# Expert results of a decoder layer: rows scattered by token on GpSimd's queue, or blocks of rows written on the weight queue and gathered at the end

## The reference, cut to what matters

```python
e_idx, gate = route(xf, w_router, b_router)      # 2 of 32 experts per token, all in one group of 4
h = jax.nn.silu(xb @ w_gate[e]) * (xb @ w_up[e])  # per expert, 1024 -> 512
y = h @ w_down[e]                                 # 512 -> 1024
y = segment_sum(y * row_gate[:, None], row_tok)   # each token: the sum of its two experts' rows
x = layer_norm(DEEPNORM_ALPHA * x + y, ln_g[l, 2], ln_b[l, 2])
```

## Time and profile before

| | |
|---|---|
| time, median of 3 runs | 1139.21 us (1138.52 to 1142.39) |
| span of the profiled execution (its first to its last instruction) | 1135.4 us; its time with what lies around the span isn't given apart |
| TensorE busy | 1058.4 us, 93% of the span |
| DVE, ACT, POOL busy | 345.5, 273.6, 85.8 us |
| SP's queue (q1) | 252.81 MB |
| POOL's indirect DMAs (q0) | 8.40 MB |
| HBM read, written | 257.60 MB, 13.05 MB |

### The profile page before, as it was taken

How to read it: one execution, slowest core, us unless ns; L and a number is a source line. 1 busy time by engine, 2 the same in 40 slices (tenths; PEclk the granted TensorE clock), 3 DMA queues, 4 the chain that set the end, 5 groups by cost and what they waited for, 6 DMA issues and landing times.

```text
span 1135.4 us, 15981 instructions
## 1 busy us (share of the span) xinstructions
PE 1058.4 (93%) x6710; PEld 533.3 (47%) x6710; DVE 345.5 (30%) x729; ACT 273.6 (24%) x540; POOL 85.8 (8%) x133
## 2 busy tenths in 40 slices
PE   9999999999899999999998999999998898898896
PEld 4444455566655544566446544444443333333332
DVE  0179522334664453104146211111111011011116
ACT  2431122234454500023202211222111011011123
POOL 2000100000000000100000211111111101101110
PEclk9999999999999999999999899999999989989999
DMA  8112220222024320923316999999999999999996
GB/s 278 37 41 86 97 76 2 76 76 76 14 64 149 110 77 1 361 84 117 148 74 257 368 398 404 403 394 393 393 396 392 401 395 394 399 396 401 398 401 251
DMA packets 55847, 263.31 MB, mean 232 GB/s; under 512 B 7250, under 2 KB 8402, under 8 KB 30944
## 3 DMA queue, kind: packets, MB, share of 16 engines
q1 hardware_dynamic: 49424, 252.81, 57.8%
q0 software_dynamic: 5120, 8.40, 2.3%
q10 hardware_dynamic: 1232, 1.07, 0.3%
HBM read 257.60 MB, written 13.05 MB: 238 GB/s over the span
## 4 chain that ended last, share of the span: by engine, by line
PE 31%; DMA 24%; DVE 3%; issue 1%; ACT 1%; SPq 0%; POOLq 0%; ACTq 0%; DVEq 0%
DMA ring<-in_w_exp_up 7%; PE cpair L2020 5%; PE bank L2030 5%; PE tpair L2020 4%; DMA ar<-in_w_exp_up 3%; PE bank L1861 2%; PE bank L1841 2%; DMA mixT<-in_w_exp_down 2%; DMA ring<-in_w_exp_down 2%; DMA avq<-in_w_exp_up 2%; PE tpair L1861 1%; PE bank L1834 1%; PE cpair L1861 1%; PE tpair L1841 1%; PE cpair L1841 1%; DMA mixT<-y_rows 1%
## 5 line engine op out<-in xcount | busy, mean ns | idle before, releaser
L2020 PE MATMUL cpair<-ring,xgT 128*64 128x512 f32 x312 | 82.8, 594 | 7.6 <-DMA ring<-in_w_exp_up 4.4
L2234 ACT ACTIVATE hs<-cpair 64x512 f32<-64x512 f32 x21 | 12.4, 589 | 237.7 <-PE cpair L2020 237.7
L2464 DVE SCALAR_TENSOR_TENSOR ye<-bank,tabs,xgt 128x512 f32<-128x512 f32 x30 | 22.5, 751 | 136.0 <-PE bank L2030 136.0
L2030 PE MATMUL bank<-ring,hT 128*64 128x512 f32 x224 | 57.6, 656 | 6.2 <-DVE hT L2454 6.2
L2450 DVE TENSOR_TENSOR hs<-cpair,hs 64x512 f32<-64x512 f32 x21 | 14.6, 693 | 154.3 <-ACT hs L2234 154.3
L922 PE MATMUL bank<-xT,ring 128*128 128x512 f32 x128 | 60.9, 606 | 0.0
L1776 POOL DMA_INDIRECT y_rows<-ye,tabs x30 | 30.3, 1011 | 383.8 <-DVE ye L2464 383.8
L2020 PEld LDWEIGHTS cpair<-ring,xgT 128*64 128x64 f32 x312 | 26.2, 137 | 53.1 <-issue 52.0
L365 PE MATMUL bank<-xT,ring 128*128 128x512 f32 x112 | 48.5, 593 | 0.0
L2241 ACT ACTIVATE xgt<-xgt,tabs 64x512 f32<-64x512 f32 x64 | 46.0, 719 | 1.6
L2020 PE MATMUL tpair<-ring,xgT 128*64 128x512 f32 x152 | 39.5, 594 | 4.5 <-DMA ring<-in_w_exp_up 2.5
(11 more groups left out here) (471 smaller groups left out, 1894.7 us busy)
## 6 DMA issues: line engine op xcount, KB each, us to landing
ring<-in_w_exp_gate SPq DMA_DIRECT2D x30, 1024.0 KB, 11.1
ring<-in_w_exp_down SPq DMA_DIRECT2D x30, 1024.0 KB, 11.1
ring<-in_w_exp_up SPq DMA_DIRECT2D x28, 1024.0 KB, 11.2
ring<-in_w_in SPq DMA_DIRECT2D x6, 2048.0 KB, 8.1
ring<-in_w_mem_kv SPq DMA_DIRECT2D x4, 2048.0 KB, 10.3
mixT<-in_w_exp_down SPq DMA_DIRECT2D x7, 1024.0 KB, 10.3
ar<-in_w_exp_down SPq DMA_DIRECT2D x7, 1024.0 KB, 11.0
xT<-in_w_exp_gate SPq DMA_DIRECT2D x6, 1024.0 KB, 11.5
```

The lines of the kernel that those rows point to most:

```text
L2020: last = nc.tensor.matmul(bank[b][m * CAP:(m + 1) * CAP, :], xgT[:, k, :], w(m, h)[:, j * DE:(j + 1) * DE], start=(k == 0), stop=(k == KT ...
L2030: last = nc.tensor.matmul(bank[b][m * CAP:(m + 1) * CAP, :], ht[:, k, :], w(2, h)[:, o:o + 512], start=(k == 0), stop=(k == FT - 1))
```

## The change

The result of an expert no longer goes to the rows of its tokens. The 64 rows of expert e go as they are, empty slots too, to rows 64e to 64e+63 of a table `y_first` in DRAM, by two direct DMAs on SP's queue (`result_out`, 64 partitions x 512 values each, 256 KB together). They are issued in SP's loop over the pieces: the result of e-1 after the piece that takes the place of the third piece of expert e, that is after piece 6e+2+23. The result of 26 is the last in the loop; those of 27, 28 and 29 follow the loop. y_out now counts 32 for each result. The token's own rows of the last two experts go the same way (`token_rows_out`).

At the end POOL gathers the two rows of each token: eight indirect DMAs of 128 rows of 4 KB, by an index `slot_at` = 64 x expert + place (plus a term for further passes, if there were any), which DVE computes during routing. SP only loads the norm's parameters. The table `tabs` becomes `toks` and `gates`; the column of rows goes, and the factor ALPHA is now carried through the one-hot products instead of being derived from the row.

```diff
-        def row_and_gate_columns(pe, ls):
+        def gate_columns(pe, ls):
...
-        def rows_and_gates_read(dve, ls, n):
+        def gates_read(dve, to, n):
             dve.wait_ge(tab_full, 2 * n)
-            nc.vector.tensor_scalar(tabs[:, :, 1], bank[7][:, 0:NE], ls.row_off[:, 0:1], None, ALU.add)
-            nc.vector.tensor_scalar(tabs[:, :, 3].bitcast(F32), bank[7][:, 0:NE], 2.0 * S - 2.0 * OFF, ALPHA, ALU.is_lt,
-                                    ALU.mult)
-            nc.vector.tensor_copy(tabs[:, :, 2].bitcast(F32), bank[7][:, NE:2 * NE]).then_inc(tabs_done, 1)
+            nc.vector.tensor_copy(to[:, :, :].rearrange("p f e -> p (f e)"), bank[7][:, 0:2 * NE]).then_inc(tabs_done, 1)
...
         def rows_out(eng):
             for s in range(2):
-                eng.wait_ge(y_out[s], 16 * (LAST - 1) // 2)
+                eng.wait_ge(y_out[s], 32 * (LAST - 1) // 2)
...
+                    def result_out(e):
+                        sp.wait_ge(y_scaled, e + 1)
+                        for h in range(2):
+                            sp.dma_start(y_first[e * CAP:(e + 1) * CAP, h * 512:(h + 1) * 512], ye[half[h], e % 2, :])\
+                                .then_inc(y_out[e % 2], 16)
+                    def token_rows_out(e):
+                        sp.wait_ge(x_done, 2 * (e + 1))
+                        for h in range(2):
+                            sp.dma_start(y_first[e * CAP:(e + 1) * CAP, h * 512:(h + 1) * 512], xrow[half[h], e % 2, :])\
+                                .then_inc(late_out, 16)
+                    sent = 0
...
                         sp.wait_ge(w_read, read_at[e, DN if i == 2 else GU, h])
                         piece_here(sp, n - 4)
                         load_piece(sp, n)
+                        if i == 0 and h == 1 and sent < e < LAST:
+                            result_out(e - 1)
+                            sent = e
+                    for e in range(sent, LAST - 1):
+                        result_out(e)
...
-                    rows_out(sp)
-                    sp.wait_ge(late_out, 32)
+                    for e in PE_LAST:
+                        token_rows_out(e)
                     down_read(sp, LAST - 2)
                     sp.wait_ge(f_end, more * NE + 1)
-                    for t in range(NT):
-                        if t == 2:
-                            for h, src in enumerate((ln_g, ln_b)):
-                                sp.dma_start(ln3[:, h, :], src[0, 2:3, :].to_broadcast([P, D])).then_inc(n3.here, 16)
-                        sp.dma_start(yb[t], y_v[t * P:(t + 1) * P, :, :]).then_inc(y_read[t], 16)
+                    for h, src in enumerate((ln_g, ln_b)):
+                        sp.dma_start(ln3[:, h, :], src[0, 2:3, :].to_broadcast([P, D])).then_inc(n3.here, 16)
...
                     for e in range(LAST - 1):
                         rows_in(e + 2)
-                        pool.wait_ge(y_scaled, e + 1)
-                        scatter(tabs[:, e, 1:2], ye[:, e % 2, :]).then_inc(y_out[e % 2], 16)
...
-                    further_blocks(pool, before, body)
-                    for e in PE_LAST:
-                        pool.wait_ge(x_done, 2 * (e + 1))
-                        scatter(tabs[:, e, 1:2], xrow[:, e % 2, :]).then_inc(late_out, 16)
+                    further_blocks(pool, before, body, after)
+                    rows_out(pool)
+                    pool.wait_ge(late_out, 64)
+                    down_read(pool, LAST - 2)
+                    for t in range(NT):
+                        for k in range(TOP_K):
+                            r = k * NT + t
+                            collect(yb[t][:, k, :], y_first[:, :], SLOTS, slot_at[:, r:r + 1]).then_inc(y_read[t], 16)
...
@@ routing, DVE
                     dve.wait_ge(oh_both, 2)
+                    link(dve, V.tensor_tensor(ohr[:, :, :, :], oh[:, 0:TOP_K, :, :],
+                                              ls.erow[:, :].unsqueeze(1).unsqueeze(1).to_broadcast(wide), ALU.mult))
+                    link(dve, V.tensor_reduce(slot_f[:, :], ohr[:, :, :, :].rearrange("p k t e -> p (k t) e"), AX_X,
+                                              ALU.add))
                     dve.wait_ge(rk_full, 1)
...
-                    tokens_read(dve, 1)
+                    rows = TOP_K * NT
+                    link(dve, V.tensor_tensor(past[:, :, :], ls.thresholds[:, :].unsqueeze(1).to_broadcast([P, rows, S // CAP - 1]),
+                                              ls.place[:, :].unsqueeze(2).to_broadcast([P, rows, S // CAP - 1]), ALU.is_le))
+                    link(dve, V.tensor_tensor(slot_f[:, :], slot_f[:, :], ls.place[:, :], ALU.add))
+                    tokens_read(dve, toks, 1)
+                    link(dve, V.tensor_reduce(blk_of[:, :], past[:, :, :], AX_X, ALU.add))
+                    link(dve, V.scalar_tensor_tensor(slot_at[:, :], blk_of[:, :], float(NE * CAP - CAP), slot_f[:, :], ALU.mult,
+                                                     ALU.add))
...
@@ experts, DVE
                         if e >= 2:
-                            dve.wait_ge(y_out[e % 2], 16 * (e // 2))
+                            dve.wait_ge(y_out[e % 2], 32 * (e // 2))
```

More of the change, by code:

```diff
@@ L1387, in hybrid_decoder_trunk @@
         class Lists:
-            KEPT = 905
+            KEPT = 904
             def __init__(self, flat):
@@ L1404, in hybrid_decoder_trunk @@
         lists_out, lists_back, asked = sem("lists_out"), sem("lists_back"), sem("asked")
-        tabs = sb("tabs", [P, NE, 4], I32)
+        toks = sb("toks", [P, NE], I32)
+        gates = sb("gates", [P, 2, NE])
         hits_done, tab_full, tabs_done = sem("hits_done"), sem("tab_full"), sem("tabs_done")
@@ L1566, in hybrid_decoder_trunk @@
         combT = sb("combT", [P, 2, S])
-        y_rows = nc.dram_tensor("y_rows", (TOP_K * S * 2, D // 2), F32, kind="Internal").ap()
+        SLOTS, FURTHER = NE * CAP, (S // CAP - 1) * NE * CAP
+        y_first = nc.dram_tensor("y_first", (SLOTS, D), F32, kind="Internal").ap()
+        y_further = nc.dram_tensor("y_further", (FURTHER, D), F32, kind="Internal").ap()
+        y_half_rows = y_further.rearrange("r (h c) -> (r h) c", h=2)
         n3 = Norm(2)
@@ L1595, in hybrid_decoder_trunk @@
         ls2 = Lists(free[8])
+        toks2 = free[9][:, 0:NE].bitcast(I32).rearrange("p (e i) -> p e i", i=1)
+        gates2 = free[9][:, NE:3 * NE].rearrange("p (f e i) -> p f e i", f=2, i=1)
         acc = ((6, 7), (3, 1), (2, 4), (5, 0))
@@ L1607, in rows_out, with further_blocks @@
             for s in range(2):
-                eng.wait_ge(y_out[s], 16 * (LAST - 1) // 2)
-        def further_blocks(eng, before, body):
+                eng.wait_ge(y_out[s], 32 * (LAST - 1) // 2)
+        def further_blocks(eng, before, body, after=None):
             n = eng.value_load(more_i[0:1, 0:1], min_val=0, max_val=S // CAP - 1)
@@ L1616, in further_blocks @@
                     body(blk)
+                if after:
+                    after()
             return n
@@ L1689, in before @@
                         sp.dma_start(ls2.kept, kept_rows[:, :]).then_inc(lists_back, 16)
+                        sp.wait_ge(f_cleared, 1)
+                        for b in range(S // CAP - 1):
+                            sp.dma_start(y_further[b * NE * CAP:(b + 1) * NE * CAP, :].rearrange("(r p) c -> p r c", p=P),
+                                         xf.unsqueeze(1).to_broadcast([P, NE * CAP // P, D])).then_inc(f_zero, 16)
+                        sp.wait_ge(f_zero, 16 * (S // CAP - 1))
                     def body(blk):
@@ L1781, in rows_in @@
                         pool.wait_ge(x_done, 2 * (e - 1))
-                        gather(xg[half[e % 2], :], tabs[0:CAP, e, 0:1]).then_inc(xg_here[e % 2], 16)
-                    gather(xg[half[1], :], tabs[0:CAP, 1, 0:1]).then_inc(xg_here[1], 16)
+                        gather(xg[half[e % 2], :], toks[0:CAP, e:e + 1]).then_inc(xg_here[e % 2], 16)
+                    gather(xg[half[1], :], toks[0:CAP, 1:2]).then_inc(xg_here[1], 16)
                     pool.wait_ge(tabs_done, 1)
@@ L2241, in first_rows @@
                             nc.scalar.activation(xrow[half[h], e % 2, :], xg[half[e % 2], h * 512:(h + 1) * 512], ACT.Copy,
-                                                 scale=tabs[half[e % 2], e, 3:4].bitcast(F32)).then_inc(x_done, 1)
+                                                 scale=gates[half[e % 2], 1, e:e + 1]).then_inc(x_done, 1)
                     def unscaled(e):
-                        act.wait_ge(y_out[e % 2], 16 * (LAST - 1) // 2)
+                        act.wait_ge(y_out[e % 2], 32 * (LAST - 1) // 2)
                         down_read(act, e)
@@ L2441, in routing @@
                     combination(0)
-                    rows_and_gates_read(dve, ls, 1)
+                    gates_read(dve, gates, 1)
                     combination(1).then_inc(comb_done, 1)
```

97 lines of the change are left out of this document (67 added, 30 removed).

## The result

The changed kernel takes 1163.42 us (median of 4 runs, 1160.39 to 1165.34), the kernel before 1140.13 us beside it. The ratio is 1.0198, with a 95% interval from 1.0176 to 1.0220: slower by 2.0%. The forecast was 1169 us, its range 1157 to 1185. The profiled execution took 1162.13 us with a span of 1160.4 us, 25.0 us longer than that of the kernel before.

The account below looks back on a forecast made before the run. The DMA engines' weight stream was taken as the bound; the down product of expert 29 ending 29.9 us later, -1.0 at the end and +0.9 for the clock gave +29.8 us: 1169 us, range 1157 to 1185.

Parts of the forecast that it names:

- Steps 1 to 3: Weight stream: piece 187 at 1099.5 us, plus 18.2 us for 26 writes, less 9.9 for 31 scatters, lands at 1107.8.
- Step 3: Behind piece 187: result 26 needs its own 0.7 us and 1.3 us for the end of a write, landing at 1109.8.
- Step 4: Down product of expert 29: DVE L2464 0.75 us and semaphores 0.2, start 1110.7, end 1114.4 instead of 1084.5, +29.9 us.
- step 6: Clock in the last experts: a stretch at the lower level would cost 1.7 us, even odds, +0.9 us.
- Step 5: Kernel end: the eight gathers are covered by TensorE's work by about 6 us and its 1.0 us wait goes, -1.0 us.
- Rival E: Kernel end: the eight gathers are slow, DVE waits 14 us for the fourth token tile, 1183 us; chance 12%.
- Step 7: Routing: six small DVE instructions more, 0.4 us left ahead of the gates, hidden by the stock of weights: 0.
- Rival B: SP's queue: the result doesn't stand in line, landing in 7.1 us (1164 us) or 2.6 us (1159 us); chance 15%.

Follow-up runs that it names:

- the kernel with two scatters: The kernel before with each scatter of an expert's result issued twice, the second to a table nobody reads: 1153.97 us, ratio 1.0123 to the kernel before.
- the best version with direct writes: The changed kernel with ACT issuing results 0 to 28 and the last token rows, result 29 on SP behind piece 188: 1144.69 us, 1.0039 of the kernel before.
- the kernel with DVE's other order: The changed kernel with DVE's two hidden-row instructions of expert e+1 ahead of the one that waits for ye: 1192.96 us, ratio 1.0462 to the kernel before.

## Why the prediction was right, and where its terms were off

**The mechanism** is as forecast. The result stands in line behind pieces 184 to 187, DVE waits for it from the sixth expert on, and the down product of 29, for which 1079.13 had been enough, must wait. Let ACT issue the results and 18.7 of 23.3 us go; move the result three pieces in SP's order and 7.7 us move. Holding the scatters back costs 15.5 us too, but by way of late gathers. The lateness has two parts. DVE's row for the result of 26 in the changed kernel:

```profile
1068.26 0.75 DVE L2530 SCALAR_TENSOR_TENSOR ye<-bank,gates,xgt 128x512 f32<-128x512 f32 x1 [13.07 <-DMA y_first<-ye]
```

It is written at 1069.01 us, its second half leaves at 1090.68 and has landed at 1101.05: 21.7 us until its turn in SP's program has come, and 10.4 us of landing. On ACT's queue the landing is 6.1 to 6.7 us. So standing in line behind the pieces is worth some 4 us, an estimate from these numbers, and the turn the rest; no run moved the one without the other.

DVE's recorded waits are 13 us, not the 2 to 3 us an expert that the forecast named, because they count DVE's own idle time. What an expert loses is some 3 us (16.6 less 13.47), and only while the kernel before still lived on its stock.

**Steps 1 to 3, the landing of piece 187: 1107.8 us forecast, 1100.5 measured** (1092.30 + 8.49 less 0.33). This is the mis-sized term, 7.3 us too much. 26 x 0.61 = 15.9 us stands where 18.2 was taken, and 29 x 0.45 = 13.1 us where 9.9 was taken; that makes +2.8 instead of +8.3. The changed kernel took 2.65 us less from piece 31 to piece 187 than the one before, which leaves 5.4 us that these two prices don't explain. Other kernels differ by about as much with the same bytes: the one with late scatters took 428.30 us (656.30 to 1084.60) where the kernel before took 434.33, and the three with results on ACT took 434.3 to 434.7 where the changed kernel took 431.68. I leave it open. Against that, the changed kernel reaches piece 31 3.7 us later; 1.8 us of it were there at the first piece of ring, at 577.95 instead of 576.19 us, ahead of all that the change touches.

**Step 3, the landing of the result: 2.0 us behind piece 187 forecast, 0.6 measured** (1101.1 less 1100.5), so its own 0.6 us at the rate of the stream is all that shows, and the end of a write was not on top of it. 1.4 us too much. The Trainium skill (DMA: Bandwidth & Descriptors, "Latency and other measured facts") has about 2 us of fixed cost for a DMA and would have added still more than the row's 1.3 us; the trace agrees with neither here: the result lands 0.6 us behind the piece.

**Step 4: DVE L2464 and 0.2 us forecast, 3.1 us measured** from 1101.13 to 1104.25. The step missed what is queued behind the waiting instruction on its engine. `hs` and `hT` of the next expert stand behind it on DVE and TensorE's transposes wait for them: 28.8 us in all within the stream, 2.2 us at the end. The product then ran at the lower clock for the most part, 6.26 us and not 3.65; step 6 had 0.9 us for that. Together 3.9 us too little (2.2 + 2.6 less 0.9).

**Step 5, the end: -1.0 us forecast, -1.0 measured.** The gathers go out 1.3 us apart, and end under TensorE's work:

```profile
1127.07 1.02 POOL L1810 DMA_INDIRECT xT<-y_first,blkones  x1 [38.18 <-DMA y_first<-xgt]
1128.40 1.00 POOL L1810 DMA_INDIRECT xT<-y_first,blkones  x1 [0.30 <-issue]
...
1136.18 0.99 POOL L1810 DMA_INDIRECT mixT<-y_first,blkones  x1 [0.30 <-issue]
```

Rival E falls, and plain reads in their place change nothing that can be told.

**Step 7, routing at nothing.** The stock does not hide a later start of a stream that from then on runs at the rate of the DMA engines. How much the six small instructions delay it, can't be told: from the first piece of ring to piece 31 the kernel before took 78.2 us, the changed one 80.2, the kernel with two scatters, whose routing is the old one, 81.1 (578.38 to 659.51).

What is around the span was 1.7 us (1162.13 less 1160.4) and not 3.8; the other runs of the kernel before have 1.7 to 2.1 us, so the 3.8 set a median against the span of a faster execution. So 1169 is 7.3, 1.4 and 2.1 us too high and 3.9 too low: 6.9 us, down to the 1162.1 of the profiled execution. That the time lies in the forecast's own 1162 to 1177 us, near its lower end, owes something to luck: the largest term was 8.3 us where 1.0 was measured, and a term that was missing made up for half of it.

**Rival B** gave the same time, 1159 to 1164 us, by a mechanism that isn't there: the result lands after 10.1 us, and moving it in the queue moves the time. The rule of the Trainium skill behind it (the same page, "Issuing engines are not separate DMA queues"), that the issuing engine saves only the time of issuing, does not hold in this kernel for a single small write: the same writes land in 6.1 us from ACT and in 10.1 us from SP. The 16 us by which that kernel was faster are not all of this kind, since its results also leave sooner.

**Still open** are some 4.5 us (0.39%) between the best version with direct writes and the kernel before. Its profile has a start of the stream 3.6 us later and a wait of 3.1 us at the end; neither was taken away alone.

## What to carry to other kernels

A small write that frees a buffer does not belong on the queue of a stream of large loads: it costs the stream only its bytes, but it leaves only when its turn in the issuing engine's program has come, lands behind everything ahead of it, and whoever waits for the buffer waits for both. Count how many transfers stand ahead of it and by how many experts the buffers cover that, and then what is queued behind the waiting instruction on its own engine. A stock of weights hides such a lag in the middle and not at the end, where nothing is left to catch up with.

## What the runs showed of the hardware

- Beside a stream at about 400 GB/s a scatter that moves 0.13 MB in rows of 2 KB costs the stream 0.45 us, and a direct write of 0.26 MB in rows of 2 KB 0.61 us. By the byte the write is the cheaper one; by the expert it is not, because it carries the empty slots too. GpSimd's busy time goes from 85.8 to 60.5 us.
- With up to four 1 MB pieces in flight ahead of it on SP's queue, a write of 128 KB lands after 10.1 us in the median (8.7 us in the kernel with the result three pieces earlier), the pieces themselves after 10.6 to 11.1; from ACT's queue on the same 16 engines it lands in 6.1 to 6.7 us beside them. How the engines share themselves between the queues no row shows.
- In the kernel with DVE's other order a wait of 1.35 us ahead of the down product was followed, from 721 us on in every expert, by 6.43 us for its 16 matmuls and not 3.65, at a granted clock of 0.82 over the stream: the wait and what came with it are 4.1 us, three times the wait. The first four of these waits, of the same length, were followed by 3.65 to 5.35 us.
